# Moving the parts of x by 16, 48 and 28 bytes inside each partition of the on-chip memory, in a two-block float32 transformer kernel

## The reference, cut to what matters

```python
# first block: mixer (MoBA attention and HGRN2), cross attention, gated network
z = rmsnorm(x) @ w_in                      # 1024 x 9216, split into nine groups
x = x + (o_attn @ w_br_attn ... o_hgrn @ w_br_hgrn) @ w_out
x = x + memory_cross_attention(rmsnorm(x), mem, wq_x, wkv_x, wo_x)
x = x + swiglu(rmsnorm(x), w_ffn_in, w_ffn_out)     # hidden width 2816
# second block, two layers (NSA attention, then differential attention)
x = x + 0.5 * swiglu(rmsnorm(x), ffn1_w_in, ffn1_w_out)
x = x + mixer(rmsnorm(x))
x = x + 0.5 * swiglu(rmsnorm(x), ffn2_w_in, ffn2_w_out)
```

## Time and profile before

| | |
|---|---|
| runs of the kernel | 1646.16 us median of 3 (1645.43 to 1646.96) |
| the profiled execution | 1647.38 us, span from first to last instruction 1645.6 us |
| TensorE busy | 1623.2 us, 99%, 11554 matmuls |
| loads of the stationary operand | 1467.6 us, 89% |
| VectorE busy | 1220.4 us, 74% |
| ScalarE busy | 927.8 us, 56% |
| GpSimd busy | 152.0 us, 9% |
| DMA | 283.82 MB, mean 172 GB/s |
| granted TensorE clock | 0.997 of full speed |

### The profile page before, as it was taken

One profiled execution on the slowest core, in us unless ns is written; L12 is line 12 of the kernel. 1 busy time (PEld: TensorE's weight loads), 2 busy tenths in 40 slices (PEclk: granted clock), 3 DMA queues, 4 the chain that ended last, 5 costly groups with the idle time before them and its releaser, 6 DMA issues.

```text
span 1645.6 us, 27290 instructions
## 1 busy us (share of the span) xinstructions
PE 1623.2 (99%) x11554; PEld 1467.6 (89%) x11554; DVE 1220.4 (74%) x1482; ACT 927.8 (56%) x1249; POOL 152.0 (9%) x63
## 2 busy tenths in 40 slices
PE   8999999999999999999999899999999999999999
PEld 8999989999988888888987598888888898898888
DVE  6888868665588767986578958876888667778864
ACT  6966778455554445444488854444544447864442
POOL 0000000000022101220000002210122000002210
PEclk9999999999999999999999899999999999999999
DMA  7554434544355455555552225546554564245544
GB/s 273 181 189 155 155 128 145 189 168 167 140 208 188 147 190 201 205 180 176 201 180 104 103 103 207 199 142 216 209 181 171 172 223 153 103 163 209 183 159 132
DMA packets 44618, 283.82 MB, mean 172 GB/s; under 512 B 4944, under 2 KB 6608, under 8 KB 17744
## 3 DMA queue, kind: packets, MB, share of 16 engines
q1 hardware_dynamic: 44352, 281.99, 48.4%
q10 hardware_dynamic: 144, 0.08, 0.0%
HBM read 281.00 MB, written 1.05 MB: 171 GB/s over the span
## 4 chain that ended last, share of the span: by engine, by line
PE 92%; DVE 4%; ACT 3%; issue 1%; DMA 0%; ACTq 0%; DVEq 0%
PE bank L526 91%; ACT WH L1238 1%; DVE WL L1842 1%; DVE STAT L2005 1%; PE bank L708 1%; ACT SB L1366 1%; DVE SB L2002 0%; DMA PAR<-in_par 0%; DVE FB L2002 0%; DVE FB L2376 0%; PE bank L1174 0%; ACT PT L1381 0%; ACT FB L1375 0%; ACT TMP L1425 0%; ACT XR L1245 0%
## 5 line engine op out<-in xcount | busy, mean ns | idle before, releaser
L1842 DVE TENSOR_TENSOR WL<-RAW,WH 128x2048 fp32r<-128x2048 f32 (+2 forms) x280 | 585.2, 2093 | 165.1 <-ACT WH L1238 161.3
L1238 ACT ACTIVATE WH<-RAW 128x2048 fp32r<-128x2048 f32 (+2 forms) x280 | 490.1, 1754 | 309.9 <-PE bank L526 305.9
L526 PE MATMUL bank<-XR,WH 128*128 128x256 f32 (+1 forms) x2608 | 645.7, 326 | 0.5 <-DVE WL L1842 0.5
L526 PE MATMUL bank<-XR,WL 128*128 128x256 f32 x1832 | 515.0, 281 | 0.0
L526 PEld LDWEIGHTS bank<-XR,WH 128*128 128x128 f32 x2608 | 435.9, 188 | 46.2 <-issue 3.6
L526 PEld LDWEIGHTS bank<-XR,WL 128*128 128x128 f32 x1832 | 345.7, 189 | 0.1
L526 PE MATMUL bank<-XF,WH 128*128 128x512 f32 x880 | 305.3, 392 | 0.0
L526 PE MATMUL bank<-XM,WH 128*128 128x512 f32 (+1 forms) x928 | 279.1, 362 | 0.0
L526 PE MATMUL bank<-XF,WL 128*128 128x256 f32 x880 | 246.0, 280 | 0.0
L526 PE MATMUL bank<-XM,WL 128*128 128x256 f32 x800 | 223.8, 280 | 0.0
L526 PEld LDWEIGHTS bank<-XF,WH 128*128 128x128 f32 x880 | 165.2, 188 | 36.5
(11 more groups left out here) (296 smaller groups left out, 1759.6 us busy)
## 6 DMA issues: line engine op xcount, KB each, us to landing
RAW<-in_f1i SPq DMA_DIRECT2D x44, 1024.0 KB, 4.8
RAW<-in_f2i SPq DMA_DIRECT2D x44, 1024.0 KB, 4.8
RAW<-in_w_in SPq DMA_DIRECT2D x35, 1024.0 KB, 4.8
RAW<-in_w_ffn_in SPq DMA_DIRECT2D x22, 1024.0 KB, 4.8
RAW<-in_f1o SPq DMA_DIRECT2D x32, 704.0 KB, 4.1
RAW<-in_f2o SPq DMA_DIRECT2D x32, 704.0 KB, 4.2
RAW<-in_diff_w_in SPq DMA_DIRECT2D x12, 1024.0 KB, 4.9
RAW<-in_w_ffn_out SPq DMA_DIRECT2D x16, 704.0 KB, 4.1
```

Source lines behind the costliest of these rows:

```text
L526: return e.matmul(o, l, r, start=start, stop=stop)
L1238: e.activation(split_at(u, cols)[0], RAW[:, u % NRAW, 0:cols], ACT.Copy).then_inc(hi_done.tick(u), 1)
L1842: e.tensor_tensor(lo, RAW[:, u % NRAW, 0:cols], hi.bitcast(f32), sub).then_inc(lo_done.tick(u), 1)
```

## The change

A helper `parts_of` cuts the two parts out of a flat tensor, some words behind its start. XR starts 4 words (16 bytes) later in its tensor, XM and all of FA 12 words (48 bytes), and XF, XS, XV, XO and all of FB 7 words (28 bytes). XW gets no shift. Since a tensor that has grown pushes those behind it, with starts rounded up to 32 bytes, the addresses after are: WH 41088 and WL 65664 as before, XR 91312, HT to STAT each 32 bytes further, XM and FA 142192, XW 158592, FB, XF and XS 175004, XV 191388, XO 199580. By 64 the remainders are now 48 (XR), 48 (XM), 0 (XW) and 28 (XF, XS, XV, XO), in place of 32 for all. No instruction is added, removed or moved on any engine: the order, the shapes and the waits are the same; only the addresses differ.

```diff
+        def parts_of(buf, at, n):
+            return buf[:, at:at + 2 * n].rearrange("p (z c) -> p z c", z=2)
+
...
-        XR = sb("XR", [128, 2, 2048], f32r)
+        XR = parts_of(sb("XR", [128, 4096 + 4], f32r), 4, 2048)
...
-        with nc.sbuf_tensor("XM", [128, 2, 2048], f32r) as XM:
-            with nc.sbuf_tensor("XW", [128, 2, 2048], f32r) as XW:
-                pass
-        FA = sb("FA", [128, NA * 2048])
-        with nc.sbuf_tensor("XF", [128, 2, FF * 2], f32r) as XF:
-            pass
-        with nc.sbuf_tensor("XS", [128, 2, 2048], f32r) as XS:
-            pass
+        with nc.sbuf_tensor("XM", [128, 2 * 2048 + 12], f32r) as below_xw:
+            XM = parts_of(below_xw, 12, 2048)
+            with nc.sbuf_tensor("XW", [128, 2 * 2048], f32r) as xw:
+                XW = parts_of(xw, 0, 2048)
+        FA = sb("FA", [128, NA * 2048 + 12])[:, 12:12 + NA * 2048]
+        with nc.sbuf_tensor("XF", [128, 4 * FF + 7], f32r) as xf:
+            XF = parts_of(xf, 7, 2 * FF)
+        with nc.sbuf_tensor("XS", [128, 2 * 2048 + 7], f32r) as xs:
+            XS = parts_of(xs, 7, 2048)
...
-            with nc.sbuf_tensor("XV", [128, 2048], f32r) as XV:
-                pass
+            with nc.sbuf_tensor("XV", [128, 2048 + 7], f32r) as xv:
+                XV = xv[:, 7:7 + 2048]
...
-            with nc.sbuf_tensor("XO", [128, 2, 2048], f32r) as XO:
-                pass
-        FB = sb("FB", [128, NB * 2048 + 1024 + 2048])
+            with nc.sbuf_tensor("XO", [128, 2 * 2048 + 7], f32r) as xo:
+                XO = parts_of(xo, 7, 2048)
+        FB = sb("FB", [128, NB * 2048 + 1024 + 2048 + 7])[:, 7:7 + NB * 2048 + 1024 + 2048]
```

## The result

| | before | after |
|---|---|---|
| runs side by side, median | 1646.56 us of 4 (1645.43 to 1648.22) | 1658.7 us of 4 (1658.43 to 1659.64) |
| the profiled execution's span | 1645.6 us | 1656.6 us |
| granted TensorE clock | 0.997 | 0.998 |

The ratio is 1.0072, with a 95% interval of 1.0059 to 1.0084. The change makes the kernel 0.7% slower, 12.1 us. The forecast was 1629 us and faster; its sign is wrong.

A forecast was written before the change was run, and what follows sets the result against it. The prediction took TensorE, through the number of matmuls times their start-to-start time, to bound the kernel. Half of a 34 us gain, 17 us, with other engines and DMA at 0, gave 1646.2 - 17 = 1629 us, range 1600 to 1662 us.

The forecast's parts named there:

- What bounds the kernel: Whole kernel: TensorE, busy 1623.2 of 1645.6 us, sets the time; VectorE (74%) and ScalarE (56%) are not the bound.
- the ground on which the change acts: All f32r matmuls: no instruction or wait changes, so the effect is only in durations of instructions whose operands moved.
- The bounds, 0 and 83 us: All f32r matmuls: gain between nothing and 83 us (1563 us) if the new places removed all excess; loss unbounded.
- 12.5 + 7: f32r records: about 12.5 ns too long for 512 columns and about 7 ns for 256, against plain float32.
- If the median went to the best seen, the gain would be 34 us ... I take half of that, 17 us.: f32r matmuls: 7176 x 4 ns + 2640 x 2 ns = 34 us; half taken by choice, a 17 us gain.
- The other engines and DMA, 0 us each: ScalarE and VectorE on XF and FB tiles, DMA on RAW and small FB loads: slack covers any slowing, cost 0.
- nothing happens: Rival, all f32r matmuls: the excess is a fixed price, low address bits don't matter; 1646 us, chance 0.27.
- slower, through the odd word of FB: Rival, XF, XS, XO and XV: starts 28 bytes past a multiple of 64 cost 14 us; 1660 us, slower 0.23.
- The rule of 16-byte lines: Moved buffers: a penalty per line crossing; XR and XM stay, FB buffers get one line more per run; no time given.
- Much faster: Rival, all f32r matmuls: two streams hit the same place together, the shift removes most of 83 us; 1563 to 1605 us, 0.08.
- The range: Whole kernel's time, for 8 in 10: 1600 us to 1662 us, leaving out the largest gains and larger losses.

## Why the prediction was wrong, point by point

*What bounds the kernel* was right: the span went with the matmuls, and no other engine or wait took part. So was the ground on which the change acts. The single-buffer kernels show it: each moved buffer changes its own matmuls and leaves the large groups of the others within 1 ns. What XR's pairs pay hangs on the rest as well: 350.0 ns with XR alone moved, 346.7 and 351.1 in after.

*The bounds, 0 and 83 us.* The 83 us took the whole excess over half the pace of plain float32 as something that a place could remove. The least pair of 15 other placements is 343.3 ns, 3.4 ns under the 346.7 of before, and the least 256 is 113.4 ns, 4.6 under. No placement had both. A bound by an ideal that no row shows said nothing of what can be reached. Nor do its terms fit the prediction's own starts: a pair was 346.5 ns against 320 of columns, 26.5 over, where the records gave 12.5 + 7.

*"If the median went to the best seen, the gain would be 34 us ... I take half of that, 17 us."* This is the step that failed, twice over.
- It took the spread of records within a form as a scale on which the median sits near the slow end, so that a move could hardly do harm. But XF's 256 records did go from a median of 280 to 277 ns, as that step wanted,

```profile
L530 PE MATMUL bank<-XF,WL x880: 276/277/278, 565.5 to 1653.3; 128*128 128x256 f32 x176
```

  and its pair went from 346.7 to 348.7 ns. The record's length is not the interval from start to start. The prediction had said ahead of the sum that the time goes from start to start, and then summed records.
- It gave the sign by a choice. Nothing in the trace of before says whether the old place is among the good or the bad ones; one place per buffer was all it held. Of the 15 other placements, pairs ran at 343.3 ns in parts of two, at 346.7 in all or parts of ten, and at 348.7 to 359.8 in parts of 13. Thirteen kernels came out slower (five of them by one run only), one the same and one 0.1% faster: before was among the good. The term measured +11.2 us where -17 stood.

*The other engines and DMA, 0 us each:* right. VectorE's busy time rose by 0.9 us, ScalarE's by 0.4, and no wait of TensorE by more than 0.3 us. The Trainium skill's ratio of 1.30 to 1.05 ns a column for pairs of words that start on an odd one ("Vector Engine (DVE) Microarchitecture Reference", "Measured stream behaviour on trn2") is not seen in runs of 128 words and more: VectorE's writes of 512 numbers to XF take 686 ns for 685, and those to FB 693 for 691.

*The rival "nothing happens"* argued that since pairs in XR and XF read alike, the higher address bits don't matter, and that WH moving against XR stationary reads as the reverse. The first inference was wrong: with the weights moved by 32 bytes, XR (160) and XM (32) part at 346.7 and 352.0 ns. That two places read alike against one place of the weights doesn't say that they do against another. So was the second: with all x at a multiple of 64, the 256s with XR stationary went from 118.3 to 114.8 ns and those with XR moving from 117.2 to 117.6.

*The rival "slower, through the odd word of FB"* gave 1660 us. That it lies near the 1658.7 measured is luck: its mechanism fell. It priced XF at 7.0 us and XS and XO at 6.7, with XR and XM free. Measured in after: XF +1.8, XS and XO -1.4, XR +6.7, XM +4.1 us. The kernel with FB alone is 1.0008. The rule of 16-byte lines named beside it ("SBUF — State Buffer", "Door 1: The DMA port swizzle" of the Trainium skill), by which XR and XM, shifted by whole lines, would stay, is spoken against by the kernels with XR alone (1.0053) and XM and FA alone (1.0032).

*"Much faster"* fell with all runs.

*The range* of 1600 to 1662 us held the time only through that rival's price, so by the same luck.

**What stays open.** That the loss is in the places of XR, XM and XF, and how much each pays, is shown. No rule was found that gives the interval from the places. Distance by up to 128 bytes, own place alone and the remainder by 64 each fell; distance by 256 bytes is untested. Three of the kernels (after, and the two with WL at 64 and WH at 128 that came first) run the same pairs from the same addresses at two values in different networks. After's pattern came back in a second execution, so the program seems to fix it, but what in the program does was not found. A candidate is the phase in which a network's stream of matmuls starts: that XF's value goes with the input half before it in two kernels speaks for this, but in after it is 348.7 ns whatever comes before, and no run set that phase by itself. The bank of the result memory that a matmul writes to is another candidate, and no run varied it.

## What to carry to other kernels

When TensorE is the bound, with matmuls of 256 and 512 columns and a fresh stationary operand for each, moving a buffer by some bytes can matter: here it cost up to 1.4% (by one run) and gained at most 0.1%. Treat a change of addresses, padding for another purpose included, as a change that must be timed. The trace of one placement does not tell whether it is a good one, so a forecast of such a move has its chances on both sides. Sum intervals from start to start, never lengths of records, and look at more than one stage: a mean can hide a pattern, and the same addresses another value.

## What the runs showed of the hardware

- A pair of 512 and 256 f32r columns, with a fresh stationary operand each, takes 343.3, 346.7, 350.0 or 353.3 ns on the mean of a network, in some cases 348.7, 351.1, 352.0 or another value up to 359.8, at a granted clock of 1.00. At 2.4 GHz the first four are 824, 832, 840 and 848 cycles, for 768 columns. The Trainium skill ("TensorE: Matmul & The Clock Gate", "Back-to-back issue gap") gives N / 2.4 + 2.5 ns for a matmul taken by itself, without its load, 325 ns for such a pair by an estimate from it; no placement came below 343.3.
- Single pairs need not take the mean. They fall into a short pattern that repeats through the network: all alike within 3 ns before, 354 and 346 ns in turn with XR alone moved, five pairs of 344 to 358 ns that sum to 1.76 us in the kernel with WL at 64 and all x at 32.
- The value depends on the places of x and of the weights together, and on both runs of the 512 columns. Places 128 bytes apart gave the same beside the weights of before (after's XR aside) and different ones with WL moved. It doesn't follow DMA traffic: the windows at 568 and at 578 matmuls above have the same 195 to 197 GB/s.
- Matmuls of 256 columns in a row take 113.4 to 121.0 ns by the places, and like other places than pairs do: beside the weights of before, with x at 64, they are at their best (113.4 to 114.0 ns on XM) and pairs at 353.3.
- The same addresses can give two values in one execution (346.7 and 351.1; 343.3 and 352.0; 353.3 and 346.7).
